# Attention packs of a hybrid decoder layer: the last projection unit of a pack moves between its transposes and the scores made two packs ahead

## What is computed

```python
(q, kv, gate, z_a, q_g, k_g, v_g, a_low, z_b, merge) = jnp.split(h @ w_in, _split_offsets(), axis=-1)

def masked_softmax(s, mask):
    s = jnp.where(mask, s, NEG_INF)
    p = jnp.where(mask, jnp.exp(s - jnp.max(s, axis=-1, keepdims=True)), 0.0)
    return p / jnp.maximum(jnp.sum(p, axis=-1, keepdims=True), TINY)

def attend(q, k, v, bias, mask):
    scale = q.shape[-1] ** -0.5
    s = jnp.einsum('...qgrd,...kgd->...grqk', q.astype(F32), k.astype(F32)) * scale + bias
    p = masked_softmax(s, mask)
    o = jnp.einsum('...grqk,...kgd->...qgrd', p, v.astype(F32))
    return o, p

o_nsa = gate[:, :, 0, :, :, None] * o_cmp + gate[:, :, 1, :, :, None] * o_slc + gate[:, :, 2, :, :, None] * o_win
```

## Time and profile before

| | us |
|---|---|
| median of 3 runs (1350.97 to 1353.65) | 1353.49 |
| the profiled execution | 1351.7 |
| its span in the trace | 1349.9 |
| TensorE busy | 1280.1 (95%) |
| VectorE busy | 666.8 (49%) |
| ScalarE busy | 559.2 (41%) |
| GpSimd busy | 120.7 (9%) |
| TensorE busy over 382 to 847.4 us (the pack loop and its lead) | 449.5 of 465.4 |

### The profile page before, as it was taken

How to read it: one execution, slowest core, us unless ns; L and a number is a source line. 1 busy time by engine, 2 the same in 40 slices (tenths; PEclk the granted TensorE clock), 3 DMA queues, 4 the chain that set the end, 5 groups by cost and what they waited for, 6 DMA issues and landing times.

```text
span 1349.9 us, 22855 instructions
## 1 busy us (share of the span) xinstructions
PE 1280.1 (95%) x9229; PEld 1159.8 (86%) x9229; DVE 666.8 (49%) x1352; ACT 559.2 (41%) x1025; POOL 120.7 (9%) x154
## 2 busy tenths in 40 slices
PE   5999998999999989999999999899979989999998
PEld 4999998999988879899989999788856779999876
DVE  6202145655845554544334443577678666443342
ACT  6212236533455444453333333564467554332221
POOL 2100001103300000000002000212000350000000
PEclk9999999999999999999999999899999989999999
DMA  7251453422522112222222222555254846452231
GB/s 207 63 171 42 119 144 110 142 74 62 80 64 69 54 43 64 64 74 64 64 64 80 64 64 64 179 162 155 78 197 152 279 150 189 138 158 67 101 128 58
DMA packets 156905, 145.22 MB, mean 108 GB/s; under 512 B 27360, under 2 KB 141360, under 8 KB 156736
## 3 DMA queue, kind: packets, MB, share of 16 engines
q1 hardware_dynamic: 154016, 135.33, 33.2%
q0 software_dynamic: 2784, 8.43, 2.1%
HBM read 105.88 MB, written 41.88 MB: 109 GB/s over the span
## 4 chain that ended last, share of the span: by engine, by line
PE 62%; DVE 7%; ACT 5%; issue 2%; DVEq 0%; another core or an unknown queue 0%; ACTq 0%
PE ps L240 36%; PE ps L2567 7%; PE ps L1690 4%; PE ps L1729 4%; PE ps L1706 4%; ACT sP L2283 1%; DVE sP L2057 1%; DVE sP L2036 1%; PE ps L2474 1%; PE ps L2442 1%; DVE pPT L2045 1%; PE ps L2575 1%; PE ps L1637 1%; PE ps L2533 1%; ACT gjunk L2883 1%
## 5 line engine op out<-in xcount | busy, mean ns | idle before, releaser
L240 PE MATMUL ps<-hH,wH 128*128 128x352 f32 (+1 forms) x1320 | 437.8, 332 | 7.5 <-DVE stg L375 4.7
L240 PE MATMUL ps<-hH,wL 128*128 128x352 f32 (+1 forms) x1320 | 425.9, 323 | 0.0
L240 PE MATMUL ps<-hL,wH 128*128 128x352 f32 (+1 forms) x1320 | 425.1, 322 | 0.0
L240 PEld LDWEIGHTS ps<-hH,wH 128*128 128x128 f32 (+1 forms) x1320 | 248.2, 188 | 21.3 <-issue 13.6
L240 PEld LDWEIGHTS ps<-hL,wH 128*128 128x128 f32 (+1 forms) x1320 | 249.4, 189 | 2.2 <-issue 1.9
L240 PEld LDWEIGHTS ps<-hH,wL 128*128 128x128 f32 (+1 forms) x1320 | 248.0, 188 | 0.3
L227 DVE TENSOR_TENSOR wL<-w_raw,wH 128x1024 fp32r<-128x1024 f32 (+1 forms) x70 | 86.0, 1229 | 168.3 <-ACT wH L219 168.0
L2283 ACT ACTIVATE sP<-sP,stat 128x640 f32<-128x640 f32 (+7 forms) x128 | 92.8, 727 | 90.8 <-DVE stat L2036 90.6
L360 ACT ACTIVATE stg<-ps 128x352 f32<-128x352 f32 x132 | 60.7, 461 | 147.8 <-PE ps L240 147.0
L2045 DVE COPY pPT<-ps 128x512 f32<-128x512 f32 (+1 forms) x71 | 45.5, 651 | 140.5 <-PE ps L1706 140.0
L219 ACT ACTIVATE wH<-w_raw 128x1024 fp32r<-128x1024 f32 (+1 forms) x70 | 73.5, 1049 | 70.5 <-issue 39.5
(11 more groups left out here) (391 smaller groups left out, 1899.6 us busy)
## 6 DMA issues: line engine op xcount, KB each, us to landing
w_raw<-in_w_in SPq DMA_DIRECT2D x61, 512.0 KB, 3.9
p_spill<-stg SPq DMA_DIRECT2D x132, 176.0 KB, 1.8
zt<-p_spill SPq DMA_DIRECT2D x24, 528.0 KB, 4.6
w_raw<-in_w_in SPq DMA_DIRECT2D x17, 256.0 KB, 3.9
gvT<-p_spill SPq DMA_DIRECT2D x8, 528.0 KB, 4.9
x_all<-in_x_prompt SPq DMA_DIRECT2D x8, 512.0 KB, 10.0
m_raw<-in_w_branch_b SPq DMA_DIRECT2D x8, 512.0 KB, 5.4
xr<-in_x_prompt SPq DMA_DIRECT2D x8, 512.0 KB, 3.7
```

The lines of the kernel that those rows point to most:

```text
L240: mm = nc.tensor.matmul(ps[0:t.m, bank, 0:NF], w[:, c % 2, t.m * k:t.m * k + t.m], x[n][:, k, :], start=(k == 0 and i == 0), stop=(k == t. ...
```

## The change

Only TensorE's order in the pack loop is changed. The units of a pack but the last come first, then the transposes, then the last unit (`pe_units(pe)` runs one), then the scores and the values as before. The other engines' code is untouched.

```diff
@@ -1833,9 +1833,10 @@
             scores(2)
             scores(3)
             for M in range(NS0):
-                pe_units(pe, units_at(M))
+                pe_units(pe, units_at(M) - 1)
                 transposes(2 * M)
                 transposes(2 * M + 1)
+                pe_units(pe)
                 scores(2 * M + 4)
                 if M < NS0 - 1:
                     scores(2 * M + 5)
```

## The result

| | before | after |
|---|---|---|
| median of the runs shown side by side | 1352.38 us (4 runs, 1350.97 to 1353.65) | 1328.97 us (4 runs, 1326.87 to 1330.19) |
| the profiled execution, its span | 1351.7, 1349.9 | 1326.9, 1325.1 |
| TensorE busy | 1280.1 | 1271.3 |

The ratio is 0.983, 95% interval 0.981 to 0.984. The changed kernel is faster by 23.4 us between the medians and by 24.8 between the two profiled executions; the prediction had 18.5. What failed is the size of four terms, above all of the waits on gating.

What follows compares the result with a forecast made beforehand. TensorE was taken as the bound, with 62% of the chain that ended last. Terms summing to 18.5 us took the profiled 1351.7 to 1333.2; from the median of 1353.5 the forecast was 1335.0 us, range 1331 to 1345.

Steps and rivals of the forecast that it cites:

- gating waits: Pack loop: four TensorE waits of a projection unit for an earlier unit's gated result all go, 4.66 us gained.
- clock at M = 5: Scores and values of pack M = 5: TensorE's clock no longer falls to half speed behind the wait, 0.78 us gained.
- changes of kind: TensorE's switches between units, transposes and scores in each pack: -2.7 to +4.3 us over 27 packs, taken as 0.
- five waits of 0.66: Packs M = 7, 8, 16, 17, 25: the moved unit covers the scores' waits for VectorE's copies, 3.30 us gained.
- M = 5, copies: Scores of pack M = 5: of the 3.98 us wait for copies 0.15 stays, 3.83 us gained.
- passage up to the gate product, with M = 26's 0.85: Passage to the last head: loss falls from 4.1 to 1.7 us with issue gaps kept, 2.4 us gained.
- clock in the passage: Passage to the last head after M = 26: TensorE's half clock goes, 2.7 us gained, or 0.
- (1): Passage gives only its 0.85 us: page loads still starve TensorE, clock falls again; gain 14.25, 1339.2 us; chance 0.16.
- (1b): Only the clock falls again in the passage, transposes holding it no more than idleness; gain 15.8, 1337.7 us; chance 0.12.
- (2): Changes of kind on TensorE cost their upper bound, 4.3 us, without or with (1): 1339.3 to 1343.5 us; chance 0.12.
- (3): Pack loop: the edit only moves waits from before scores to before transposes; 1350 to 1354 us, no change; chance 0.06.
- (4): Slower: transposes wait in every pack for VectorE's scores; at 1 us in each of 27 packs, 1362 us; chance 0.06.

## Right and wrong, step by step

The mechanism was right, and sizes failed: the sum has 22.6 us measured where 18.5 were predicted. Of the difference of 4.1 us 1.4 is in the gating waits, 0.7 in the clock at M = 5, 1.2 in the changes of kind and 0.8 in the passage.

| term of the sum | predicted | measured | |
|---|---|---|---|
| five waits of 0.66 | 3.30 | 3.36 | right |
| four gating waits | 4.66 | 6.06 | mechanism right, size wrong |
| M = 5, copies | 3.83 | 3.77 | right |
| M = 10, copies | 0.88 | 0.95 | right |
| M = 0 | 0 | 0, a wait of 1.79 where 2.0 was forecast | right |
| passage up to the gate product, with M = 26's 0.85 | 2.4 | 0.88 + 2.31 = 3.19 | size wrong, the gaps didn't stay |
| clock at M = 5 | 0.78 | 1.47 | size wrong |
| clock in the passage | 2.7 | 2.61 | right |
| changes of kind on TensorE | 0 | 1.19 | within the bounds, value wrong |
| sum | 18.5 | 22.6 | |

The passage is taken in two parts, up to the gate product and from it on, because the half clock acts only behind the gate product. Up to it the kernel before takes 10.65 us from the scores of M = 26 and the changed one 836.22 - 827.88 = 8.34; from there to the last head's first key product it is 8.22 and 5.61, where the prediction had put the pure work at 5.5.

**What bounds, and what the edit removes: right.** The 14 packs with a wait or ahead of one hold 20 of the 23 us, every wait named goes but for 0.19 us at M = 5, nothing takes their place but the one at M = 0, and no engine beside TensorE becomes the bound. (The prediction counted 15 packs without a wait; it is 14, since nine wait for copies and four others for gating.) The chains that I walked come out nearly to the digit. At M = 3 in the changed kernel T is 451.19 + 1.91 = 453.10 and VectorE's last score ends at 462.24 = T+9.1 (T+9.3 forecast); at M = 4, T = 470.35, it ends at 480.92 = T+10.6 (as forecast), 0.94 us ahead of the transposes that need it:

```profile
462.16 0.08 DVE L2037 DVE_READ_ACCUMULATOR2_ANT stat<- 128x1 f32 x1
...
480.85 0.07 DVE L2037 DVE_READ_ACCUMULATOR2_ANT stat<- 128x1 f32 x1
...
481.86 1.91 PE L1706 MATMUL ps<-ident,sP 128*128 128x128 f32 x16
```

The first two are VectorE's timeline, the third TensorE's.

**The gating waits: the step that failed first.** The term had 4.66 us and measured 6.06. I summed the idle in brackets, against my own rule that the distance between starts is what a stretch costs. Two rows of the kernel before around the wait at M = 4, the last matmul ahead of it, and the second behind it:

```profile
472.21 0.32 PE L240 MATMUL ps<-hH,wL 128*128 128x352 f32 x1
...
474.83 0.32 PE L240 MATMUL ps<-hL,wH 128*128 128x352 f32 x1
```

Between them stands the row at 474.57 with its idle of 2.03. In a running unit these three starts span 0.32 us; here 2.62, so the wait costs 2.3, not 2.03. The modelled end of a pipelined matmul (0.32 long, though the next starts after 0.16) eats 0.16 of the idle, and the first matmul after a pause is followed only after 0.26. Times four that is 1.1 us; the rest of the 1.4 is the 0.06 that these packs gain like all others, within 0.1. The waits for copies don't show it: 0.66 in the row, 3.36 / 5 = 0.67 in the period.

**The clock: mis-sized, and told by one execution.** At M = 5 I took the pure work from a pack with larger scores, 3.83 us, where it is 3.18, so the fall cost 1.43 and not 0.78. I also read "behind 2.22 us it stays up" as a property of the kernel. It is one draw: behind waits of about 2 us it fell in 9 of 24 cases. In its three profiles the kernel before pays for three or four episodes in the packs and the passage, about 4 to 6 us, the changed one for none in two profiles. The profile that I worked from had three. The Trainium skill, "TensorE: Matmul & The Clock Gate", Part 4, had spoken against taking the passage's clock back, since a transpose of TensorE's transpose mode doesn't count as activity. By that rule the changed kernel would have kept the loss of 2.6 us. It didn't: over the passage the granted clock is 1.00 in all six profiles that have the edit in M = 26. From 834.28 to 836.22, eight transposes and 0.90 of idle, are 1.94 us, and yet behind 1.66 to 1.77 us of plain idle at M = 3 the clock fell in half of the cases. The transposes at M = 0 of the kernel before point the same way: with the 2.22 behind them they make 4.1 us, more than the 3.8 in the passage (1.04 and 2.77), and yet the clock fell in two of nine there and in seven of eight here. The rows lean against the rule for these transposes of 128x128 float32. They don't refute it, since what ran ahead of the two places differs too.

**The passage.** The step that failed is that the issue gaps stay: no profile with the edit has them, nor have six of the seven with pack 26 and the page loads as before. The 3.3 us that I had noted for "without the gaps" is near the 3.19 measured. That it is near is in part luck, for 0.44 of it is ScalarE's pause, which the prediction didn't see.

**The changes of kind.** I had bounds of -2.7 to +4.3 us and took the middle. Measured are 0.06 us of gain in each pack and 0.15 more in some, 1.19 over the 13 periods in which nothing else happens, inside the bounds. Sixteen transposes and then a unit, a sequence that no row of before had, in the changed kernel:

```profile
483.53 0.41 PE L240 MATMUL ps<-hH,wH 128*128 128x352 f32 x1
```

They take 483.53 - 481.86 = 1.67 us where they took 1.91 ahead of scores, 0.24 less. The moved unit takes 520.47 - 516.43 = 4.04 up to the scores where a unit in a run takes 3.87, so that 0.17 goes back.

**The range.** Its lower end took in the bounds of two terms and held the others for exact. All larger errors were on one side: idle that is under-reported, a fall of the clock undercounted, and 2 us outside the packs by which any two executions differ. From 1335.0 to the measured 1329.0 it is 6.0 us: 4.1 in the terms above, 1.1 because the median of before is 1352.4 over four runs and was 1353.5 over three, and 0.8 left over. With an end for the gating waits from the starts (1.4 more) and one more episode of half clock (1.6) it would have stood at about 1328.

**The rivals.** (1) and (1b) didn't happen. (2) has the wrong sign. (3) is what one pack alone does (M = 5, and M = 0 in the changed kernel). (4) doesn't happen with one unit, and does with two where the next pack has two.

## What to carry to other kernels

When an engine waits in several consecutive steps of a software pipeline, follow the chain that releases it back through the steps before: here the edit at the largest wait gained least of all, and the one a step earlier took over three quarters of that wait away (3.98 to 0.85 us). Price a wait by the distance between starts around it, compared with the same instructions where nothing waits, not by the idle that a row shows. And take what a wait does to TensorE's clock from several executions: a short wait has the price of its own length, and by chance that of a half-speed stretch behind it.

## What the runs showed of the hardware

The same wait of 2.2 us ahead of the same twelve matmuls left the granted clock at 1.00 in seven profiles and dropped it to 0.50 in two; one of 2.0 us dropped it in three of seven, one of 3.9 in seven of seven. With the DMA engines at a share of 1.08, TensorE's eight transposes in the changed kernel's passage took 1.04 us, without a gap. And sixteen transposes cost 0.24 us less ahead of a projection unit than ahead of scores.
